# Half a row block on both halves of the partitions: two column blocks of a down projection side by side in TensorE's array

## What is computed

```python
D_MODEL, SEQ, D_FF = 1024, 256, 2752          # first block
def swiglu(h, w_gate, w_up, w_down):
    return (jax.nn.silu(h @ w_gate) * (h @ w_up)) @ w_down
x = x + 0.5 * swiglu(rms_norm(x, ffn1_norm), ffn1_w_gate, ffn1_w_up, ffn1_w_down)
...                                           # Fourier mixer, grouped attention, w_out
x = x + 0.5 * swiglu(rms_norm(x, ffn2_norm), ffn2_w_gate, ffn2_w_up, ffn2_w_down)
...                                           # second block: conv, memory attention, two more
                                              # feed-forward layers of width 2816 = 22 * 128
```

## Time and profile before

| | us |
|---|---|
| median of 3 runs | 1269.14 |
| the three runs | 1267.29, 1269.14, 1270.62 |
| the profiled execution, its own time | 1268.03 |
| its span in the trace | 1266.2 |
| mean granted clock of TensorE | 0.994 |
| busy in the span: PE, PE's weight loads, DVE, ACT | 99%, 87%, 73%, 52% |
| DMA share of the 16 engines' time | about 50% |

### The profile page before, as it was taken

How to read it: one execution, slowest core, us unless ns; L and a number is a source line. 1 busy time by engine, 2 the same in 40 slices (tenths; PEclk the granted TensorE clock), 3 DMA queues, 4 the chain that set the end, 5 groups by cost and what they waited for, 6 DMA issues and landing times.

```text
span 1266.2 us, 18117 instructions
## 1 busy us (share of the span) xinstructions
PE 1251.6 (99%) x7458; PEld 1107.5 (87%) x7458; DVE 924.1 (73%) x1291; ACT 657.7 (52%) x867; POOL 31.1 (2%) x23
## 2 busy tenths in 40 slices
PE   8999999999999999999999999999999999999997
PEld 7888888978888887888888888889998888888886
DVE  7887856587877855898658877659977657877843
ACT  6655544365655543455546555445555445555532
POOL 0000000000000000341000000000000000000000
PEclk9999999999999999999999999999999999999999
DMA  8565753224555663454436555653444543555650
GB/s 306 186 218 198 234 174 137 89 100 149 202 185 197 207 214 111 166 200 171 162 116 250 170 196 181 218 199 134 160 141 167 195 137 134 200 200 180 197 188 34
DMA packets 51298, 221.74 MB, mean 175 GB/s; under 512 B 4336, under 2 KB 5648, under 8 KB 30736
## 3 DMA queue, kind: packets, MB, share of 16 engines
q1 hardware_dynamic: 51072, 220.51, 50.4%
q10 hardware_dynamic: 144, 0.07, 0.0%
HBM read 219.52 MB, written 1.05 MB: 174 GB/s over the span
## 4 chain that ended last, share of the span: by engine, by line
PE 92%; DVE 6%; ACT 1%; issue 1%; DMA 1%; SPq 0%; DVEq 0%; ACTq 0%
PE bank L396 48%; PE bank L426 20%; PE bank L400 7%; PE bank L417 4%; PE bank L465 2%; DVE wt L1137 2%; PE bank L668 2%; PE bank L696 2%; PE bank L442 1%; PE bank L468 1%; DVE xn L1146 1%; DVE x L1151 1%; PE bank L501 1%; PE bank L447 1%; DVE x L1152 1%
## 5 line engine op out<-in xcount | busy, mean ns | idle before, releaser
L1137 DVE TENSOR_TENSOR wt<-raw,wt 128x2048 fp32r<-128x2048 f32 x202 | 464.1, 2299 | 71.9 <-ACT wt L814 71.3
L814 ACT ACTIVATE wt<-raw 128x2048 fp32r<-128x2048 f32 x202 | 386.0, 1911 | 125.6 <-PE bank L400 98.7
L396 PE MATMUL bank<-xn,wt 128*128 128x512 f32 x1712 | 418.3, 394 | 4.2 <-DVE xn L1146 3.5
L396 PEld LDWEIGHTS bank<-xn,wt 128*128 128x128 f32 x1712 | 314.8, 189 | 66.9 <-DVE xn L1146 5.6
L396 PE MATMUL bank<-h,wt 128*128 128x512 f32 (+1 forms) x1024 | 253.7, 394 | 0.0
L426 PEld LDWEIGHTS bank<-xn,wt 128*128 128x128 f32 x1856 | 240.6, 193 | 9.3
L426 PE MATMUL bank<-xn,wt 128*128 128x256 f32 x1856 | 244.1, 284 | 0.0
L396 PEld LDWEIGHTS bank<-h,wt 128*128 128x128 f32 (+1 forms) x1024 | 185.9, 188 | 39.0 <-issue 4.0
L1235 DVE TENSOR_TENSOR scratch<-bank,rest 128x512 f32<-128x512 f32 x98 | 67.6, 690 | 85.7 <-ACT rest L826 85.6
L890 ACT ACTIVATE h<-scratch 128x256 fp32r<-128x256 f32 x88 | 36.9, 419 | 158.2 <-DVE scratch L1275 158.2
L826 ACT ACTIVATE rest<-bank 128x512 f32<-128x512 f32 x114 | 67.6, 593 | 69.8 <-PE bank L426 69.4
(11 more groups left out here) (186 smaller groups left out, 956.7 us busy)
## 6 DMA issues: line engine op xcount, KB each, us to landing
raw<-weights SPq DMA_DIRECT2D x158, 1024.0 KB, 4.9
raw<-weights SPq DMA_DIRECT2D x92, 512.0 KB, 4.9
k_t<-mem_t SPq DMA_DIRECT2D x2, 1024.0 KB, 8.0
raw<-weights SPq DMA_DIRECT2D x4, 256.0 KB, 5.1
x<-x_t SPq DMA_DIRECT2D x4, 256.0 KB, 5.5
out_t<-work SPq DMA_DIRECT2D x4, 256.0 KB, 2.3
v_s<-fourier SPq DMA_DIRECT2D x2, 256.0 KB, 5.2
con<-consts SPq DMA_DIRECT2D x1, 385.5 KB, 8.5
```

The costliest lines, as they stand in the source:

```text
L396: return pe.matmul(out, hi, a.rearrange("p a s -> p (a s)"), start=first, stop=False, skip_group_check=True)
L814: act.activation(wt[t % RING][:, 0], raw[t % RING][:], ACT.Copy).then_inc(weight_hi, 1)
L1137: dve.tensor_tensor(wt[t % RING][:, 1], raw[t % RING][:], wt[t % RING][:, 0].bitcast(F32), ALU.subtract).then_inc(weight_lo, 1)
```

## The change

The half row block k = 21 of `down0` and `down1` is held twice, in partitions 0 to 63 (`UPPER`) and again in 64 to 127 (`LOWER`), of h and of the weights. Of the four column blocks, the even ones are multiplied from the upper half of the array's rows and the odd ones from the lower half. In tile i = 10 the k = 21 products of all four column blocks are issued first; k = 18 to 20 follow by column block. `scaled_halves` writes each result twice, and what follows it works on 128 partitions. In the four tiles concerned (i = 5 and i = 10 of the two phases) the half tile with k = 20 and 21 comes in three transfers in place of one.

```diff
+UPPER, LOWER = slice(0, LAST), slice(LAST, P)
+SHORT = ("down0", "down1")
+HALVED = [i for i in range(FF // 2) if FF // 2 - 1 in (u for _, u in DOWN_HALVES[2 * i:2 * i + 2])]
...
-                halves = any(FIRST[d] <= u < FIRST[d] + COUNT[d] for d in DOWNS)
-                n += 0 if u < RING else 2 if halves else 1
+                down = next((d for d in DOWNS if FIRST[d] <= u < FIRST[d] + COUNT[d]), None)
+                n += 0 if u < RING else 4 if down in SHORT and u - FIRST[down] in HALVED else 2 if down else 1
...
-                        sp.dma_start(raw[slot][:, 8 * half:8 * half + 8, :].rearrange("p (k m) c -> p k m c", k=2),
-                                     weights[t0 + u].rearrange("p (k m) c -> p k m c", k=2)[:, :, 4 * d:4 * d + 4, :]
-                                     ).then_inc(landed[slot], 16)
+                        dst = raw[slot][:, 8 * half:8 * half + 8, :].rearrange("p (k m) c -> p k m c", k=2)
+                        src = weights[t0 + u].rearrange("p (k m) c -> p k m c", k=2)[:, :, 4 * d:4 * d + 4, :]
+                        if f"down{n}" in SHORT and u == FF // 2 - 1:
+                            sp.dma_start(dst[:, 0], src[:, 0]).then_inc(landed[slot], 16)
+                            for r in UPPER, LOWER:
+                                sp.dma_start(dst[r, 1], src[UPPER, 1]).then_inc(landed[slot], 16)
+                        else:
+                            sp.dma_start(dst, src).then_inc(landed[slot], 16)
...
-                def run(i, half0, d, ks, ms):
+                def rows_at(half0, ks):
+                    return [(8 * half0 + 4 * n, k) for n, k in enumerate(ks)]
+
+                def run(i, rows, d, ms, fresh=False, final=None):
                     w = wt[(t0 + i) % RING]
-                    blocks = [(8 * half0 + 4 * n + m, k, m, bank[:, 2 * PAIR[name, 2 * d + m // 2] + m % 2, :],
-                               slice(0, LAST if k == FF - 1 and n_ffn < 2 else P))
-                              for n, k in enumerate(ks) for m in ms]
+                    blocks = [(at + m, k, m, bank[:, 2 * PAIR[name, 2 * d + m // 2] + m % 2, :],
+                               (UPPER, LOWER)[m % 2] if k == FF - 1 and name in SHORT else slice(0, P))
+                              for at, k in rows for m in ms]
                     for at, k, m, out, r in blocks:
                         with_hi(out, w[r, 0, at, :], h[r, k], k == 0)
-                    if ks[0] % 4 == 2 * d and ms[0] == 0:
+                    if fresh:
                         pe.wait_ge(weight_lo, t0 + i + 1)
                     for at, k, m, out, r in blocks:
-                        mm = with_rest(out, w[r, 1, at, :], h[r, k], k == FF - 1)
-                        if k == FF - 1 and (d, m) in ((0, 1), (0, 3), (1, 1), (1, 2)):
+                        mm = with_rest(out, w[r, 1, at, :], h[r, k], k == final)
+                        if k == final and (d, m) in ((0, 1), (0, 3), (1, 1), (1, 2)):
                             mm.then_inc(acc_done, 1)
...
-                        for m in range(4):
-                            mm = run(i, 0, 1, range(FF - 4, FF), (m,))
+                        rows = rows_at(0, range(FF - 4, FF))
+                        if name in SHORT:
+                            run(i, rows[3:], 1, range(4), True)
+                            rows = rows[:3]
+                        for m in range(4):
+                            mm = run(i, rows, 1, (m,), m == 0, rows[-1][1])
...
-                    for m in range(2):
-                        r = slice(m * LAST, (m + 1) * LAST)
-                        e = dve.tensor_tensor(gu_s[j % 3][0:LAST, m, :], sum_s[r, :], r_x[r, :], ALU.mult)
+                    for m, r in enumerate((UPPER, LOWER)):
+                        for twice in UPPER, LOWER:
+                            e = dve.tensor_tensor(gu_s[j % 3][twice, m, :], sum_s[r, :], r_x[r, :], ALU.mult)
```

More of the change, by code:

```diff
@@ L571, in down @@
                     if i < FF // 4:
-                        mm = run(i, 0, 0, range(4 * i, 4 * i + 4), range(4))
+                        mm = run(i, rows_at(0, range(4 * i, 4 * i + 4)), 0, range(4), True)
                     elif i == FF // 4:
-                        run(i, 0, 0, (FF - 2, FF - 1), range(4))
+                        run(i, rows_at(0, (FF - 2, FF - 1)), 0, range(4), True, FF - 1)
                         pass_begins(1)
-                        mm = run(i, 1, 1, (0, 1), range(4))
+                        mm = run(i, rows_at(1, (0, 1)), 1, range(4))
                     elif i < FF // 2 - 1:
-                        mm = run(i, 0, 1, range(4 * i - FF, 4 * i - FF + 4), range(4))
+                        mm = run(i, rows_at(0, range(4 * i - FF, 4 * i - FF + 4)), 1, range(4), True)
                     else:
+                        rows = rows_at(0, range(FF - 4, FF))
+                        if name in SHORT:
+                            run(i, rows[3:], 1, range(4), True)
+                            rows = rows[:3]
                         for m in range(4):
-                            mm = run(i, 0, 1, range(FF - 4, FF), (m,))
+                            mm = run(i, rows, 1, (m,), m == 0, rows[-1][1])
                     mm.then_inc(tile_done, 1)
@@ L876, in gate_up @@
                 for j in range(FF):
-                    rows = LAST if n < 2 and j == FF - 1 else P
                     if j == 0:
@@ L885, in gate_up @@
                         after(t0 + j)
-                    gate = gu_s[j % 3][0:rows, 0, :]
+                    gate = gu_s[j % 3][:, 0, :]
                     out_of(act, phase, j)
@@ L889, in gate_up @@
                     act.wait_ge(whole, FF * n + j + 1)
-                    act.activation(h[0:rows, j, 0, :], gate, ACT.Copy).then_inc(h_rounded, 1)
+                    act.activation(h[:, j, 0, :], gate, ACT.Copy).then_inc(h_rounded, 1)
                     if n == 0 and 3 <= j < 3 + KP:
@@ L1266, in scaled_halves, with multiplied, rest @@
                     dve.wait_ge(taken, TAKEN[phase, j])
-                    for m in range(2):
-                        r = slice(m * LAST, (m + 1) * LAST)
-                        e = dve.tensor_tensor(gu_s[j % 3][0:LAST, m, :], sum_s[r, :], r_x[r, :], ALU.mult)
+                    for m, r in enumerate((UPPER, LOWER)):
+                        for twice in UPPER, LOWER:
+                            e = dve.tensor_tensor(gu_s[j % 3][twice, m, :], sum_s[r, :], r_x[r, :], ALU.mult)
                     e.then_inc(drained, 1)
-                def multiplied(j, rows=P):
-                    gate, up = (gu_s[j % 3][0:rows, i, :] for i in range(2))
+                def multiplied(j):
+                    gate, up = (gu_s[j % 3][:, i, :] for i in range(2))
                     dve.wait_ge(gated, FF * n + j + 1)
                     dve.tensor_tensor(gate, gate, up, ALU.mult).then_inc(whole, 1)
-                def rest(j, rows=P):
+                def rest(j):
                     dve.wait_ge(h_rounded, FF * n + j + 1)
-                    dve.tensor_tensor(h[0:rows, j, 1, :], gu_s[j % 3][0:rows, 0, :], h[0:rows, j, 0, :].bitcast(F32),
+                    dve.tensor_tensor(h[:, j, 1, :], gu_s[j % 3][:, 0, :], h[:, j, 0, :].bitcast(F32),
                                       ALU.subtract).then_inc(h_split, 1)
@@ L1300, in gate_up @@
                         after(t0 + max(j, 2))
-                    multiplied(j, LAST if short else P)
+                    multiplied(j)
                     if j:
@@ L1305, in gate_up @@
                         fold("mem", j - 4)
-                rest(FF - 1, LAST if n < 2 else P)
+                rest(FF - 1)
             def down(n, gain, name, scale, between={}):
```

## The result

The changed kernel takes 1260.32 us (median of 4 runs, 1258.98 to 1261.60) against 1268.22 for the kernel before (4 runs). The two medians lie 7.9 us apart. The ratio over all the runs is 0.9933, with a 95% interval of 0.9919 to 0.9946: 8.5 us less by it, between 6.8 and 10.3. Ten further experiments follow, one of them the same kernel again in more rounds: 1259.54 against 1268.27, ratio 0.9932 (0.9920 to 0.9944). Forecast were 7.3 us less and 1261.8, in a range of 1259.3 to 1265.6.

A forecast was written before the change was run, and what follows sets the result against it. PE, busy for 99% of the span, was taken as the bound. The terms 2 x 0.70 + 2.96 + 2.95 = 7.3 us came off the median of 1269.14, giving 1261.8, range 1259.3 to 1265.6.

The forecast's parts named there:

- The price of a change of row size: In i = 5 and i = 10, each change between 128 and 64 rows costs 0.19 to 0.20 us.
- One sign: In i = 10, one idle of 0.36 us among the loads ahead of the 64-row ones and one behind.
- The pairs: In the k = 21 groups of i = 5 and i = 10, two matmuls run together, saving 0.70 us a group.
- Rival A: In the k = 21 groups, float32r pairs don't run side by side: 4.5 us gained, 1264.6; chance 0.13.
- the estimate of 1.53: Two row tiles at 1.53x: a group saves 0.48 us in place of 0.70, the time 0.9 us longer than forecast.
- The adds' chain: Behind i = 10, DVE's adds come late and pass on 2.96 of the 3.25 us PE gains.
- PE's wait: Behind i = 10 of down0, PE waits some 0.7 us in the next phase, where it waited 0.4.
- Rival B: In the k = 21 groups, each step between upper and lower half costs 0.19 us: 1270.0; chance 0.04.
- Rival C: Behind i = 10, the adds' chain gives back more: 1.67 us saved a phase, together 3.3, 1265.8; chance 0.06.
- D: Transfers or added DVE work come on the path, once 0.85 us a phase: 1263.5; chance 0.04.
- the cover: In scaled_halves, DVE's split for i = 1 has 3.2 us of cover, 2.4 after the added operations.
- The transfers: At the begin of down0, late data for i = 5 has 9.6 us of cover, so the cost is 0.

The follow-up runs named there:

- e1_upper_only: The changed kernel with all four k = 21 column blocks on the upper half, so grouped but without pairs: 1264.38 us against 1268.67 for the kernel before.
- e3_whole_rows: The kernel before's order and transfers, but k = 21 multiplied over all 128 partitions, the lower weights zeros: 1260.99 us against 1268.67 for the kernel before.
- e4_nested: The changed kernel with the rests of k = 21 ahead of those of k = 20 in i = 5: 1259.14 us against 1268.67 for the kernel before.
- e5_uull: The changed kernel with the k = 21 column blocks in the order upper, upper, lower, lower: 1261.97 us in one execution.
- e7_four_more: The changed kernel with four more 64x256 DVE operations in each phase's scaled_halves: 1260.57 us in one execution.
- e2_old_order: The changed kernel with the order of before in i = 10, k = 18 to 21 for each column block: 1266.44 us against 1268.67 for the kernel before.
- e8: The changed kernel with twelve more 64x256 DVE operations in each phase's scaled_halves: 1269.64 us in one execution.
- e6: The changed kernel with the k = 21 group at the end of i = 10 in place of its start: 1262.69 us against 1268.18 for the kernel before.
- e9: The changed kernel with k = 21's rests first in i = 5 and, behind down0, fold 2 after rest_pair 3: 1257.81 us against 1268.27 for the kernel before.

## Why the prediction was right

**The price of a change of row size held.** I took 0.19 to 0.20 us from the excess of i = 5 and i = 10 over a whole tile. `e1_upper_only` keeps every half block on 64 rows and takes away 14 of the 16 changes in i = 10, and the group there is 1.59, the 1.39 of its matmuls and one change of 0.20; `e3_whole_rows` takes all changes away, and i = 10 falls from 8.51 to 5.6; `e4_nested` takes away two, and i = 5 falls by 0.41. One sign did not come: in i = 10 the load side was to stand idle for 0.36 us ahead of the 64-row loads, and it stood for 0.13 (the loads before end at 188.28, these begin at 188.41). So the idle of the loads, 0.36 in i = 5, is no measure of what a change costs.

**The pairs gave the full 0.70 a group.** This was the open term, as only plain float32 stood in the trace of before. The four first products on 64 rows take 0.67 us with one change of 0.20 ahead of them, so 0.47 for two pairs, and the four rests 0.23. Matmuls on 64 rows, the lists by line of the kernel with upper halves only and of the changed one (busy us, mean ns), show the same: less busy time for as many matmuls that are no shorter one by one.

```profile
L405 PE MATMUL bank<-h,wt 64*128 64x512 f32 x16 | 4.8, 417 | 0.0
```
```profile
L405 PE MATMUL bank<-h,wt 64*128 64x512 f32 x16 | 2.9, 445 | 0.0
```

A pair of 512 columns takes the 0.23 us of one. Rival A, 4.5 us, is what `e1_upper_only` built and measured at 4.2; the changed kernel is not that. The single write port of the Trainium skill (PSUM — Partial Sum Buffer, the section on the matmul accumulator) doesn't hold back a pair that writes to two banks. The measured factor of two stands against the estimate of 1.53 from the Trainium skill's figure for four tiles (TensorE: Matmul & The Clock Gate, Measured speedup vs the span model), so the estimate was the worse guide for two.

**The adds' chain**: forecast 2.96 of 3.25 us arriving, measured 3.12. DVE is late as said, with no wait between the adds. Mis-sized is only an add without a wait: m = 3 was to be added by 6.46 after the start of i = 10 and is by 6.30 (188.49 to 194.79), since I took 0.88 a bank from one that had waited. PE's wait came as forecast: counted as the prediction counts it, k = 6 at 197.15 less the start of the phase at 193.61 and 24 x 0.12, it is 0.66 us, for the 0.7 forecast. The row itself shows 0.31, and the kernel before 0.23 where the prediction counts 0.4, since its busy time reaches past the start of the last matmul.

**Rival B** is out: the group in i = 10, with 7 steps between the halves, takes 0.90 us, change of row size included, and in `e5_uull`, with 3 steps, it takes 0.90 as well (188.10 to 189.00). The prediction counted 14 steps a phase; it is 13, as L409 of k = 20 stands between the two runs of k = 21 in i = 5. At 0.19 each that is 2.5 us in place of 2.66, still more than the 2.25 of A. **Rival C** too: the shift of 3.12 goes through whole. **D**: the operations are L1285, four in 1.72 us, and the two added ones cost nothing: by the start times of the matmuls the changed kernel's shift is the same ahead of and behind them, in both phases. Four more fit as well in `down0`, and all but 0.20 us in `down1` (`e7_four_more`); the prediction had worked out the cover for `down0` only. The transfers did come later: ACT rounded tile i = 5 of `down0` after a wait for them, at 149.78 in place of 148.70, with 8.8 us of cover left.

```profile
149.78 1.92 ACT L831 ACTIVATE wt<-raw 128x2048 fp32r<-128x2048 f32 x1 [3.09 <-DMA raw<-weights]
```

**The sum.** By the start times of the matmuls, the changed kernel's trace gains 0.70 and 3.12 in `down0`, 0.70 and 3.22 in `down1`: 7.7 us, of which it lost 0.36 in the first 20 us, ahead of all that was changed. The forecast of 7.3 was a little low for the two tails. The medians lie 7.9 us apart in the first measurement and 8.7 in the second, the ratios give 8.5 and 8.6, with intervals that hold 7.7. How much of that distance is the scatter of executions isn't shown; one such step of 1.5 us is the clock in `w_in` (last section), and the two profiled executions, before and changed, both had it.

## What to carry to other kernels

Look for changes between 128 and 64 rows in a stream of matmuls before looking for empty halves of the array: each costs about 0.2 us here, nearly the price of a matmul of 512 columns (0.228), so a half block among whole ones is better padded with zeros than multiplied on 64 rows. Put half blocks in one group, their first products and rests behind each other, and only then let two share the array. Ahead of a phase whose operands come from the banks, that group belongs at the start of the last tile, and what the next phase waits for belongs first in the adding engine's order.

## What the runs showed that I had not expected

TensorE's granted clock falls in two places without a stall of PE of more than 0.4 us. In `w_in`, behind 20 matmuls of two columns, two traces differ in the same work; the kernel before and `e2_old_order`, stretches of 2 us as above:

```profile
222.00:224.00 2.00, 2.00 (x14) 2.00 (x13) 1.42 (x8) 0.00 (x0) 0.00 (x0) 0.61 0.60 254
224.00:226.00 2.00, 2.00 (x12) 2.00 (x12) 0.00 (x0) 0.00 (x0) 0.00 (x0) 0.54 0.00 0
```
```profile
222.00:224.00 2.00, 2.00 (x19) 2.00 (x18) 1.07 (x6) 0.00 (x0) 0.00 (x0) 1.00 0.40 168
224.00:226.00 2.00, 2.00 (x19) 2.00 (x18) 1.61 (x2) 1.55 (x1) 0.00 (x0) 1.00 0.00 0
```

PE is busy all the time in both, but the first ran near 1.2 GHz and lost 1.5 us (by the start times of the same matmuls ahead of it and behind it). The two kernels differ nowhere in this stretch. Of the profiled executions six had this (before, after, e3, e5, e7, e8) and six not (e1, e2, e4, e6, e9 and the changed kernel run again, whose trace ends 8.25 us ahead of before in place of 7.19). In `conv_in` the clock falls in or behind the 32 sums of two columns: in the kernel before for 1.7 us of lost time (granted 0.79 and 0.78 in the two stretches of 4 us from 500 on), in e1 for 3.4 (0.67 and 0.50 from 492 on, then 0.97). The changed kernel shows both cases of the first, with and without the fall, so it isn't the change that decides; what does is not shown. Whoever compares two traces of this kernel must take such steps out before reading a difference of 1 us.
